# One layer of a hybrid decoder: waits, splits and side steps of the front, block A and attention B put elsewhere

## What is computed

```python
h = rmsnorm(x, norm_mix_g)
z = h @ w_in                               # 1024 x 3088
gq, gk, gv, gg, glr, dq, dk, dv = split(z)
log_a = log_sigmoid(glr @ w_gk2 + b_gk) / 16
S, o_g = gla_block(S, gq, gk, gv, log_a)   # 64-token blocks, exact
o_g = rmsnorm(o_g, gla_norm_g) * silu(gg)
q, k = rmsnorm(dq), rmsnorm(dk)            # by head
p = softmax(mask(q k^T / 8))               # two (q, k) pairs a head
o_d = rmsnorm((p[0] - lam * p[1]) @ dv) * (1 - lambda_init)
x = x + concat(o_g, o_d) @ w_out
h2 = rmsnorm(x, norm_ffn_g)
x = x + square(relu(h2 @ w_up)) @ w_down
```

## Time and profile before

| what | us |
|---|---|
| median of three runs | 1372.2 (1371.47 to 1374.15) |
| the profiled execution | 1378.11 |
| its span | 1376.4 |
| PE busy | 1348.7 |
| DVE busy | 902.8 |
| ACT busy | 578.2 |
| POOL busy | 393.1 |
| granted clock, mean | 0.996 |

### The profile page before, as it was taken

How to read it: one execution, slowest core, us unless ns; L and a number is a source line. 1 busy time by engine, 2 the same in 40 slices (tenths; PEclk the granted TensorE clock), 3 DMA queues, 4 the chain that set the end, 5 groups by cost and what they waited for, 6 DMA issues and landing times.

```text
span 1376.4 us, 23928 instructions
## 1 busy us (share of the span) xinstructions
PE 1348.7 (98%) x8605; PEld 1124.2 (82%) x8605; DVE 902.8 (66%) x1619; ACT 578.2 (42%) x1075; POOL 393.1 (29%) x395
## 2 busy tenths in 40 slices
PE   9999999999999999999999999999999999999998
PEld 8777878776777777776777777667999999999998
DVE  6468668836658877747667565534376665878785
ACT  7563333414545563623235241323444453434532
POOL 3647424425423544343000000000242202332130
PEclk9999999999999999999999999999999999999999
DMA  9467644444344574657486576873454564133301
GB/s 325 118 195 220 221 142 136 138 137 125 97 156 162 192 258 129 221 188 260 153 272 225 191 253 187 297 228 135 169 192 166 203 225 153 57 119 108 108 32 63
DMA packets 125544, 239.30 MB, mean 174 GB/s; under 512 B 13601, under 2 KB 46658, under 8 KB 125426
## 3 DMA queue, kind: packets, MB, share of 16 engines
q1 hardware_dynamic: 116226, 213.64, 47.3%
q10 hardware_dynamic: 9200, 24.13, 5.1%
HBM read 197.64 MB, written 40.09 MB: 173 GB/s over the span
## 4 chain that ended last, share of the span: by engine, by line
PE 82%; DVE 7%; DMA 4%; ACT 3%; issue 2%; SPq 1%; POOL 0%; ACTq 0%; DVEq 0%; POOLq 0%
PE ps L87 23%; PE ps L89 22%; PE ps L88 22%; PE ps L1553 2%; PE ps L1372 2%; PE ps L3370 2%; PE ps L1590 2%; DMA raw_dn<-in_w_down 1%; DMA kr<-in_cache_k 1%; DMA vr<-in_cache_v 1%; DVE sd L3124 1%; PE ps L1574 1%; DVE uw_l L2079 1%; DVE wl L828 1%; PE ps L423 1%
## 5 line engine op out<-in xcount | busy, mean ns | idle before, releaser
L3135 POOL TENSOR_TENSOR kr<-kr,qb 128x512 f32<-128x512 f32 x128 | 174.6, 1375 | 165.0 <-DMA kr<-in_cache_k 164.1
L87 PE MATMUL ps<-x2hB,uw_h 128*128 128x264 f32 (+1 forms) x512 | 145.2, 284 | 0.7 <-DVE x2lB L2923 0.7
L88 PE MATMUL ps<-x2lB,uw_h 128*128 128x264 f32 (+1 forms) x512 | 144.7, 283 | 0.0
L89 PE MATMUL ps<-x2hB,uw_l 128*128 128x264 f32 (+1 forms) x512 | 144.5, 282 | 0.0
L87 PE MATMUL ps<-part_h,fh 128*128 128x264 f32 (+1 forms) x448 | 127.9, 285 | 0.0
L89 PE MATMUL ps<-part_h,fl 128*128 128x264 f32 (+1 forms) x448 | 127.0, 283 | 0.0
L88 PE MATMUL ps<-part_l,fh 128*128 128x264 f32 (+1 forms) x448 | 126.9, 283 | 0.0
L2908 DVE TENSOR_TENSOR xt<-xt,ps 128x264 f32<-128x264 f32 (+1 forms) x224 | 87.3, 422 | 35.8 <-PE ps L89 35.6
L87 PE MATMUL ps<-uh,dh 128*128 128x512 f32 x256 | 105.2, 411 | 4.2 <-DVE xt L2227 1.8
L3124 DVE TENSOR_REDUCE sd<-kr 128x8 f32<-128x512 f32 x128 | 84.8, 675 | 36.1 <-POOL kr L3135 36.0
L87 PE MATMUL ps<-x2hA,uw_h 128*128 128x512 f32 x256 | 105.2, 411 | 0.0
(11 more groups left out here) (392 smaller groups left out, 3426.4 us busy)
## 6 DMA issues: line engine op xcount, KB each, us to landing
kr<-in_cache_k SPq DMA_DIRECT2D x128, 256.0 KB, 3.4
raw_up<-in_w_up_units SPq DMA_DIRECT2D x64, 512.0 KB, 4.8
vr<-in_cache_v SPq DMA_DIRECT2D x128, 256.0 KB, 3.5
raw_dn<-in_w_down SPq DMA_DIRECT2D x32, 512.0 KB, 6.5
raw_dn<-in_w_down ACTq DMA_DIRECT2D x32, 512.0 KB, 5.5
raw<-in_w_in_units SPq DMA_DIRECT2D x23, 512.0 KB, 5.8
raw_up<-in_w_out_units SPq DMA_DIRECT2D x16, 512.0 KB, 4.2
kept_up_low<-uw_l SPq DMA_DIRECT2D x14, 512.0 KB, 6.0
```

Of the source, the lines that this page charges most:

```text
L87: pe.matmul(out, lh, rh, start=first and n == 0, stop=False, skip_group_check=onto)
L88: pe.matmul(out, lh, rl, start=False, stop=False, skip_group_check=onto)
L89: ins = pe.matmul(out, ll, rh, start=False, stop=last and n == len(ks) - 1, skip_group_check=onto)
L3135: pool.tensor_tensor(k[:, :], k[:, :], qb[v // PAGES][:, :], ALU.mult).then_inc(k_multiplied, 1)
```

## The change

Seven edits, each of which moves work or waits; no arithmetic is changed.

1. `split_after`: DVE and ACT make the parts of weight unit 11 behind group 21's start, with unit 10, and not behind group 22's; on DVE the side jobs of group 22's tick therefore come first.
2. POOL's product of key page v, for v from 33 to 57, waits until DVE has summed page v - 1 (`k_used`).
3. `loadA` is advanced first at tick 75 instead of 77 of the front, and its first step no longer waits for `go_made`.
4. The parts of the first two w_out tiles (`late`) are made behind the second tick's side jobs of groups `gg` 3 and 4 on ACT and DVE, and not ahead of them.
5. In attention B DVE makes the maxima of unit n in step 2n + 1, behind the mix of n - 1, and not in step 2n + 2.
6. ACT does its side jobs ahead of `down_high` in up tiles x = 1 and 2 of the groups g = 0 and 1 of block A, and not behind it.
7. `mixload` is advanced at feed ticks 120, 122, 124 and 126, which are down ticks of group g = 6, and not at 117, 119, 121 and 123 (t1 is t0 + 60).

```diff
--- before.py
+++ after.py
@@ -126,7 +126,7 @@
 
 def split_after(g):
 
-    table = {1: [4], 2: [5], 9: [6], 11: [7], 12: [8, 9], 21: [10], 22: [11], 24: [12], 27: [13],
+    table = {1: [4], 2: [5], 9: [6], 11: [7], 12: [8, 9], 21: [10, 11], 24: [12], 27: [13],
              32: [14, 15], 33: [16], 35: [17], 41: [18, 19], 43: [20], 45: [21], 50: [22, 23]}
     return table.get(g, [])
 
@@ -680,8 +680,6 @@
                     act.wait_ge(sem("const_made"), 2)
                     act.activation(xs[:, :, 0:NS], xg[:, NTILE % 2, :, 0:NS], ACT.Copy).then_inc(sem("xs_made"), 1)
             evacuate(g)
-            if g in (START["gg"] + 3, START["gg"] + 4):
-                m["late"]["scalar"](act, g - START["gg"] - 3)
             if g == 2:
                 act.wait_ge(sem("const_loaded"), 160)
                 act.wait_ge(sem("dve_steps"), 7)
@@ -703,6 +701,8 @@
                 copy_heads(g - 2 - START["dk"] + NTILE)
             if ticks_of(g) == 2:
                 beside(TICK[g] + 1)
+            if g in (START["gg"] + 3, START["gg"] + 4):
+                m["late"]["scalar"](act, g - START["gg"] - 3)
 
 
 
@@ -937,7 +937,7 @@
         constants()
         for g in range(len(GROUPS)):
             kind, x = GROUPS[g]
-            units_first = g in (START["gv"] - 3, START["gv"] - 2, START["dk"] + NTILE)
+            units_first = g in (START["gv"] - 3, START["dk"] + NTILE)
             if not units_first:
                 beside(TICK[g])
             for r in split_after(g):
@@ -979,12 +979,12 @@
                 gkq(g)
                 if x[1] == 2:
                     gkq_sample(g)
-            if g in (START["gg"] + 3, START["gg"] + 4):
-                m["late"]["vector"](dve, g - START["gg"] - 3)
             if kind == "low" and x == 0 or kind == "dv" and x == 1:
                 sample_normed("dq" if kind == "low" else "dk")
             if ticks_of(g) == 2:
                 beside(TICK[g] + 1)
+            if g in (START["gg"] + 3, START["gg"] + 4):
+                m["late"]["vector"](dve, g - START["gg"] - 3)
 
 
 
@@ -1493,7 +1493,7 @@
     def load(sp):
 
         if part == 0:
-            for x in ("o_summed", "state_summed", "go_made"):
+            for x in ("o_summed", "state_summed"):
                 sp.wait_ge(sem(x), CHUNKS)
             sp.wait_ge(sem("level_picked"), 8 * CHUNKS)
             m["kq_stored"](sp)
@@ -1697,13 +1697,13 @@
 
         for s in range(ATTEND_STEPS):
             n, j = divmod(s, 2)
-            if part == 0 and j == 1 and n < UNITS:
-                maxima(n)
-            if 0 <= n - 1 < UNITS:
-                if part and j == 0:
-                    maxima(n - 1)
-                if j == 1:
+            if j == 1:
+                if part == 0 and n < UNITS:
+                    maxima(n)
+                if 0 <= n - 1 < UNITS:
                     mix(n - 1)
+                if part and n < UNITS:
+                    maxima(n)
             yield
 
     return {"sync": sync, "vector": vector, "tensor": tensor, "scalar": scalar, "gpsimd": gpsimd, "steps": ATTEND_STEPS,
@@ -2126,8 +2126,12 @@
                 t = KT + FT * g + x
                 if x:
                     load_down(FT * g + x + 1)
+                attention_first = g < 2 and x in (1, 2)
+                if attention_first:
+                    beside(tick + 2 * x)
                 down_high(g, x)
-                beside(tick + 2 * x)
+                if not attention_first:
+                    beside(tick + 2 * x)
                 if g == 0 and x == 0:
                     split_high(act, t + 2)
                     act.wait_ge(norm_product, 2)
@@ -3131,6 +3135,8 @@
                 pool.wait_ge(qb_in, 16 * (max(v // PAGES, first // PAGES + part) + 1))
                 i, n = pages_in(v)
                 pool.wait_ge(page_in[i], n)
+                if 33 <= v < 58:
+                    pool.wait_ge(k_used, v)
                 k = place(v)
                 pool.tensor_tensor(k[:, :], k[:, :], qb[v // PAGES][:, :], ALU.mult).then_inc(k_multiplied, 1)
             yield
@@ -3633,7 +3639,7 @@
         put("loadRA", [t0 - 1])
         put("recurA", range(t0, t0 + side["recurA"]["steps"]))
         t0 = TICK[START["dv"]] + 9
-        put("loadA", [t0 - 2, t0 + 1])
+        put("loadA", [t0 - 4, t0 + 1])
         put("attnA", [t0 + i for i in range(4)] + [t0 + 4 + i // 2 for i in range(ATTEND_STEPS - 4)])
         t0, t1, t2, t3 = TICK[START["gk"]] + 1, TICK[START["gv"]], TICK[START["dv"]] + 4, FRONT_TICKS - 1
         put("keysA", [t0 + (t1 - t0) * i // 36 for i in range(36)])
@@ -3661,7 +3667,7 @@
         put("soft", range(t1, t1 + side["soft"]["steps"]))
         put("values", range(t1 + 12, t0 + FEED_TICKS))
         put("recurB", [t0 + i for i in chain if i >= t1 + 14 - t0][:side["recurB"]["steps"]])
-        put("mixload", [t1 + 57 + 2 * i for i in range(4)])
+        put("mixload", [t0 + 120 + 2 * i for i in range(4)])
         put("mixB", [t0 + 137 + i // 2 for i in range(9)])
 
         def run(e, eng):
```

## The result

The kernel after takes 1381.6 us (median of 5 runs, 1380.15 to 1382.45), the kernel before 1372.2 in the same comparison: a ratio of 1.0055, 95% interval 1.0037 to 1.0073. An interval is 0.15 to 0.21% to either side, so the difference of two ratios is uncertain by some 0.25%, 3.4 us.

A forecast was written before the change was run, and what follows sets the result against it. TensorE's matmul stream was taken as the bound, PE busy 1348.7 of 1376.4 us. Gains of 14.15 less losses of 5.5, net 8.7, took the median from 1372.2 to 1363.5 us, range 1356.5 to 1370.

The forecast's parts named there:

- steps 2 to 4: POOL's wait, attention A's earlier loads and the later w_out splits: gains of 4.6, 4.0 and 1.2 us.
- the one hit that the forecast left: At the picks near 272: one POOL product still holding up one DVE instruction, 1.26 us.
- step 3: Attention A's first loads issued over 10 us sooner: PE's 2.24 us wait for qt and a dip go, gain 4.0.
- Step 5: Attention B's earlier maxima: 0.3 us gained in the out phase, 4.6 lost at the first up tile, 0.9 at down ticks.
- Net 0.3: Out phase: a 0.7 us hole at 436.68 goes, 0.4 lost as maxima stand ahead of an add.
- the slower rival: Maxima hold the adds at down ticks 26, 28 and 30, three holes cost 13.5 us: 1376.1, chance 0.10.
- Step 6: ACT's attention step ahead of two high parts: PE's waits of 0.6 and 0.8 us at up tiles go, gain 1.25.
- Step 1: Split 11 a group earlier: a 2.64 us hole and its dip go, 1.2 us kept, ends 0 and 4.1.
- If that chain stays where it is: Front, g_in's store, load and first picks, ended at 164.22: PE can be early by 1.2 us and no more.
- Step 7: Last mix's rows loaded a phase later: PE's 1.6 us wait for a late value page goes, gain 1.6.
- The rivals: No stall at first up tile, 1358.9, chance 0.20; front gains given back, 1368.1, 0.20; slower, 1376.1, 0.10.
- step 2: POOL's wait for the total before: the 3.1 us hole at the picks near 272 and a dip go, gain 4.6.

The follow-up runs named there:

- a_no1567: Kernel after with edits 1, 5, 6 and 7 undone, so edits 2, 3 and 4 alone: ratio 0.9931 to the kernel before.
- a_no56: Kernel after with edits 5 and 6 undone: ratio 0.9950 to the kernel before.
- a_no256: Kernel after with edits 2, 5 and 6 undone: ratio 0.9968 to the kernel before.
- a_no156: Kernel after with edits 1, 5 and 6 undone, so edits 2, 3, 4 and 7 alone: ratio 0.9932 to the kernel before, 1363.65 us.
- a_no1356: Kernel after with edits 1, 3, 5 and 6 undone, so edits 2, 4 and 7 alone: ratio 0.9949 to the kernel before.
- a_no5: Kernel after with edit 5 alone undone: ratio 0.9970 to the kernel before.
- a_res: Kernel after with SP's residual load of the next out tile issued ahead of the side step, not behind it: ratio 1.0011 to the kernel before.
- a_dl: a_no5 with DVE's low part of one up tile (group 1, tile 2) put behind that tile's relu: ratio 0.9971 to the kernel before.
- a_s11: a_no56 with DVE's split 11 behind group 21's evacuation, still ahead of group 22's key totals: ratio 0.9954 to the kernel before, 1368.2 us.
- a_m8late: Kernel after with the maxima of unit 8 alone one step later again: ratio 1.0012 to the kernel before.
- best0: Edits 2, 3, 4 and 7, with edit 5 for the out tiles' eight units only and the residual load ahead of the odd tick's side step: ratio 0.9936.

## Why the prediction was wrong, point by point

| step | forecast, us | measured, us | from |
|---|---|---|---|
| 2, 3, 4 together | −9.8 | −9.5 | a_no1567 |
| of these 2, beside edit 1 | −4.6 | −2.5 | a_no56, a_no256 |
| of these 3 | −4.0 | −2.3 | a_no156, a_no1356 |
| 7 | −1.6 | 0 | a_no156, a_no1567 |
| 1 | −1.2 | +2.5 | a_no56, a_no156 |
| 6 | −1.25 | +2.7 | a_no5, a_no56 |
| 5 | +5.2 | +11.7 | after, a_no5 |
| sum | −8.7 | +7.5 | after |

Each number that is the difference of two runs' ratios has their noise, some 3.4 us; edit 5 alone is clear of it, and the signs of 1, 2, 3 and 6 rest on the traces too. Against the forecast edit 5 is 6.5 us worse, edit 6 4.0, edit 1 3.7, edit 7 1.6 and steps 2 to 4 0.3.

*Steps 2 to 4: right in mechanism and sum.* POOL's products no longer follow each other (268.27 and 271.90, each released by a key total), DVE's pair of products that took 5.49 us takes 0.49, and PE does not wait at 272. Not even the one hit that the forecast left is there; the view of g_in, answering to the earlier trace rows, now ends at 292 ns:

```profile
L1263 DVE TENSOR_TENSOR e<-e,g_in x112: 270/284/292, 156.7 to 845.0; 128x128 f32<-128x128 f32 x112
```

The load of qt is issued at 280.54 instead of 296.18. What is smaller for step 3 by itself may be the dip: I charged 1.5 us to every hole above 2 us, and the second trace of the kernel before has this hole without one. The parts do not add up to the 9.5: 2.5 and 2.3 leave 4.7 for edit 4, forecast at 1.2, which was never undone by itself; its hole of 1.2 us at 382 is gone in all fourteen traces that have the edit. So the sum came out, and how it is shared is open.

*Step 5: right at the one place I had worked out, and too small.* "PE starts up tile 2 at about 496.8 instead of 493.67: 3.1 us" and a dip: 3.0 us and a dip, 5.9 us measured for 4.6. The sentence that failed is "In the out phase the exponentials come half a step earlier ... Net 0.3." It priced the maxima on DVE and did not follow the key total behind them to SP's queue, where the residual load of the next tile stands behind the key load: 6.0 us by a_res. For the down ticks it said 0.9 us for all, "ends 0 and 3"; some 2 were left, within its ends and within the noise. The traces show the slower rival's mechanism, a down tile held 1.3 to 1.8 us by an add, at one of the ticks it named; its price was 12.6 us, and it was not the main loss.

*Step 6: wrong cover.* It looked for the first need of the late high part at the matmul. "The high part itself comes some 2 us later; the down tiles need it over 8 us after that." PE needs it that late, but DVE's low part is the first reader, waits 1.65 us for it in a_no5, and the relu stands behind it on DVE. That this is the whole of the loss is not shown (a_dl). The cover ought to have been sought on the next engine's program.

*Step 1: the premise failed.* "If that chain stays where it is": it did not. In a_no56 it came 2.3 us later than in a_no156, and PE, earlier by the hole that went, waited for the picks in all nine traces with edit 1: 1.9 us in six of them, 1.6, 1.4 and 0.7 in the others, six times with a dip. Without edit 1 it waited there 0 to 1.1 us, once with a dip, so the forecast's slack of 1.2 was itself one trace's. The end of the range for this step, 0, excluded a loss without a reason. And the evacuation behind the splits, for which "some 0.5 us later" was taken as covered, left a hole of 1.0 to 1.6 us near 132 in seven of the nine.

*Step 7: a hole that comes and goes.* The wait of 1.6 us for a value page stands at 889 in the first trace of the kernel before; the second has one of 1.3 us at 756 instead, the kernel after one of 1.5 at 762. Holes behind DMAs of this stream move between executions; one trace was no ground for a price.

*The rivals and the range.* None was this outcome. The slower one had one mechanism at three ticks; the loss came from three edits. Edits 5 and 6 moved work ahead of other work, and the price was taken at the engine that ran it or at the last reader, with nothing in between; for edit 1 the chain that follows was taken to stay, and it did not. The rule of the Trainium skill (SBUF — State Buffer, Who interferes with whom) would have had step 2 at 4.0 for 4.6, by a second product across DVE's instructions. The kernel after has no hole at those picks and no such DVE product held in its trace, so it does not show that loss; what it shows is a POOL product held instead, 2.10 us at 271.90 beside a weight split of DVE, for 1.27 of the one before. The runs cannot tell 0.6 us.

## What to carry to other kernels

When an instruction is moved ahead of others on one engine, follow what stood behind it through each semaphore to the next queue and on: here a key total late by two maxima held up a DMA queue, and with it a load that has nothing to do with either. A price that a part loses is sought at its first reader's program order, not at the last. And where PE stands within 2 us of several chains, making one of them faster can give back little or nothing, as step 1 did, so the parts of such a change are to be timed singly: here three parts cost more than the others gave.

## What the runs showed of the hardware

The dip behind a hole is not a fixed price. PE's hole ahead of L1372 (L1375 in a_s11) at 163 to 166 was 1.90 us in six traces, and the mean granted clock of the stretch 160 to 180 differs between them (PEclk is the third number from the end). a_dl:

```profile
160.00:180.00 20.00, 18.10 (x120) 14.76 (x119) 14.98 (x37) 3.08 (x12) 7.70 (x7) 1.00 0.58 196
```

a_no56:

```profile
160.00:180.00 20.00, 18.10 (x130) 14.80 (x127) 13.49 (x32) 5.05 (x15) 5.59 (x6) 0.91 0.53 171
```

a_s11:

```profile
160.00:180.00 20.00, 18.10 (x108) 14.47 (x107) 13.38 (x32) 3.36 (x13) 5.51 (x6) 0.83 0.56 169
```

The same hole costs nothing more, or its dip once or twice. In four of the six another hole stood some 7 us ahead (0.82 us in a_dl, 1.80 in a_no56, 0.54 in a_s11, 1.34 in a_m8late), but that does not sort them: a_no5 has the 1.91 us alone and a dip, a_dl has both holes and none. So a time forecast from one trace carries, for each hole of this size, an estimated 0 to 3 us (none, one or two dips of 1.5) that belong to the execution. The runs of the kernel before show that this is part of their spread from 1368 to 1380 us: those with a mean granted clock of 0.995 took 1375.9 to 1380.3 us, those with 0.999 took 1370.6 to 1374.4; but those with 0.997 lie between 1368.4 and 1376.5, so it is not all of it.

Nor does the length sort the holes. Two of 0.84 and 0.18 us at 476 in the kernel after, with three matmuls between them and eight of one column behind, had a dip, and in best0 one of 1.20 us ahead of the same eight had none; the hole of 2.58 us in a_no5 had none, that of 1.94 at the same place in a_res had one. So the forecast's reading that holes under 2 us have no dip rested on too few rows.
